# Hybrid encoder with a mixture of experts: router logits one tile later among the output products, and gate-weight splitting and loading in other places

## What is computed

```python
mix = jnp.concatenate([o_mla, o_d], axis=-1) @ w_o
x = layer_norm(ALPHA * x + mix, ln1_g, ln1_b)            # x1
scores = jax.nn.sigmoid(xt @ w_router)                   # the logits: 768 x 16
# top-1 of 4 groups, top-2 experts inside it, gates = scores / sum
for e in range(N_EXPERTS):
    h = jax.nn.silu(xt @ w_gate[e]) * (xt @ w_up[e])
    y = y + gates[:, e:e + 1] * (h @ w_down[e])
x = layer_norm(ALPHA * x + y, ln2_g, ln2_b)
```

## Time and profile before

| | |
|---|---|
| runs | 829.7, 826.49, 824.76 us; median 826.49 us |
| profiled execution | 825.78 us |
| its span in the trace | 823.9 us (1.9 us lie around it) |
| busy in the span | PE 722.7 us (88%), weight loads 600.3 (73%), DVE 582.2 (71%), ACT 482.4 (59%), POOL 264.6 (32%) |
| DMA | 185.71 MB, mean 225 GB/s |

### The profile page before, as it was taken

How to read it: one execution, slowest core, us unless ns; L and a number is a source line. 1 busy time by engine, 2 the same in 40 slices (tenths; PEclk the granted TensorE clock), 3 DMA queues, 4 the chain that set the end, 5 groups by cost and what they waited for, 6 DMA issues and landing times. The chain is left out here.

```text
span 823.9 us, 12546 instructions
## 1 busy us (share of the span) xinstructions
PE 722.7 (88%) x3751; PEld 600.3 (73%) x3751; DVE 582.2 (71%) x970; ACT 482.4 (59%) x864; POOL 264.6 (32%) x292
## 2 busy tenths in 40 slices
PE   4999989998999699999996499999999999999830
PEld 3898878886778477767785377888887777777620
DVE  6874445555555766785775779898998888888608
ACT  3334345545554655775127157887888788887505
POOL 3133166555654232334410114132222222232101
PEclk9999999999999879999995599999999999999965
DMA  9714220222025863311835759999999999999735
GB/s 346 254 69 154 89 77 9 70 64 64 2 65 176 263 247 115 111 34 67 322 150 195 255 173 377 393 394 390 373 389 394 392 394 393 393 394 392 243 89 242
DMA packets 71912, 185.71 MB, mean 225 GB/s; under 512 B 10560, under 2 KB 26944, under 8 KB 71872
## 3 DMA queue, kind: packets, MB, share of 16 engines
q1 hardware_dynamic: 66976, 167.38, 53.0%
q0 software_dynamic: 4896, 17.83, 8.4%
HBM read 153.20 MB, written 31.98 MB: 225 GB/s over the span
## 5 line engine op out<-in xcount | busy, mean ns | idle before, releaser
L2228 DVE TENSOR_TENSOR eDl<-rawD,eDh 128x1024 fp32r<-128x1024 f32 x68 | 80.2, 1220 | 12.3 <-ACT eDh L2172 12.1
L1265 POOL TENSOR_SCALAR me<-me,mrec 128x512 f32<-128x512 f32 (+1 forms) x48 | 65.0, 1355 | 57.0 <-DVE mrec L1444 57.0
L2228 DVE TENSOR_TENSOR eUl<-rawU,eUh 128x1024 fp32r<-128x1024 f32 x68 | 78.8, 1220 | 5.0 <-ACT eUh L2172 2.6
L2228 DVE TENSOR_TENSOR eGl<-rawG,eGh 128x1024 fp32r<-128x1024 f32 x64 | 75.9, 1222 | 7.4 <-ACT eGh L2172 6.9
L2300 POOL DMA_INDIRECT acc_rows<-yg,idx_s x17 | 31.3, 1841 | 147.8 <-ACT yg L2197 147.8
L2172 ACT ACTIVATE eGh<-rawG 128x1024 fp32r<-128x1024 f32 x64 | 65.5, 1058 | 8.1 <-DMA rawG<-in_w_gate 7.2
L1071 ACT ACTIVATE pT_h<-bank 128x512 fp32r<-128x512 f32 (+1 forms) x48 | 25.3, 527 | 75.4 <-PE bank L781 75.4
L1450 DVE TENSOR_TENSOR pT_l<-bank,pT_h 128x512 fp32r<-128x512 f32 (+1 forms) x48 | 28.9, 601 | 50.6 <-ACT pT_h L1071 50.6
L2120 PE MATMUL bank<-eGh,xgT_h 128*128 128x512 f32 x136 | 56.8, 418 | 8.5 <-DVE xgT_l L2233 7.4
L2172 ACT ACTIVATE eDh<-rawD 128x1024 fp32r<-128x1024 f32 x64 | 64.0, 1055 | 0.0
L2172 ACT ACTIVATE eUh<-rawU 128x1024 fp32r<-128x1024 f32 x64 | 62.3, 1050 | 0.0
(11 more groups left out here) (323 smaller groups left out, 2114.3 us busy)
## 6 DMA issues: line engine op xcount, KB each, us to landing
rawG<-in_w_gate SPq DMA_DIRECT2D x68, 512.0 KB, 15.3
rawU<-in_w_up SPq DMA_DIRECT2D x68, 512.0 KB, 12.4
rawD<-in_w_down SPq DMA_DIRECT2D x68, 512.0 KB, 13.6
wb_raw<-in_w_in SPq DMA_DIRECT2D x8, 512.0 KB, 4.7
wo_raw<-in_w_o SPq DMA_DIRECT2D x8, 512.0 KB, 7.4
acc_rows<-ax SPq DMA_DIRECT2D x7, 512.0 KB, 2.6
xln_rows<-res SPq DMA_DIRECT2D x6, 512.0 KB, 3.8
dqk_high<-st_h SPq DMA_DIRECT2D x8, 384.0 KB, 2.3
```

Of the source, the lines that this page charges most:

```text
L1265: nc.gpsimd.tensor_scalar(e, e, mrec[:, g % NSB:g % NSB + 1], None, ALU.mult).then_inc(m_p, 1)
L2228: nc.vector.tensor_tensor(wl_[X][i][:], raw_of(X, t, i)[:], f32(wh_[X][i][:]), ALU.subtract).then_inc(s_lo[X], 1)
```

## The change

There are two `x1T` tiles (at 202 and 42 KB) and two pairs of banks, (0, 1) and (5, 6), used in turn. On PE turn_x1(t) moves to the place ahead of the products of tile t+2 for t = 0 and behind those of tile t+1 for the others, and logits(t-1) follows turn_x1(t): turn_x1(0); products of tile 2, turn_x1(1), logits(0); products of tile 3, turn_x1(2), logits(1); products of tile 4, turn_x1(3), logits(2); products of tile 5, turn_x1(4), logits(3), logits(4), turn_x1(5), logits(5). turn_x1(1) waits in addition for the last readers of banks 5 and 6 in attention.

ACT makes the high parts of gate pieces 0 to 2 before its wait for the zero rows, and that of piece 3 behind the router's exponential and the last `ax`. DVE makes the low part of piece 0 between the two adds of tile 4, that of piece 1 between those of tile 5, that of piece 2 behind the layer norm of tile 5, and that of piece 3 behind `gate_vals`, at the very end of the block. SP issues pieces 0 to 2 of the second expert and 0 to 2 of the third, and then piece 3 of the second expert and, once that has landed, piece 3 of the third. Numbers of instructions and bytes stay as they are.

```diff
--- before.py
+++ after.py
@@ -381,7 +381,8 @@
     ln1g_sb = at("ln1g_sb", 30, [P, D])
     ln1b_sb = at("ln1b_sb", 34, [P, D])
     ax = [at(f"ax{i}", (38, 198)[i], [P, D]) for i in range(2)]
-    x1T = at("x1T", 202, [P, KD, P])
+    x1T = [at(f"x1T{i}", (202, 42)[i], [P, KD, P]) for i in range(2)]
+    X1_BANKS = ((0, 1), (5, 6))
 
     raw = {X: [at(f"raw{X}{i}", 78 + 16 * n + 4 * i, [P, 2 * FF]) for i in range(4)] for n, X in enumerate("GUD")}
 
@@ -1674,16 +1675,15 @@
                 sp.wait_ge(s_stored[i], 16 * (NT // 2))
             sp.wait_ge(s_x1st, 16 * NT)
 
-            for i in range(4):
-                sp.wait_ge(s_lo["G"], i + 1)
-                sp.dma_start(unit_dst("G", i), unit_src("G", 1, i)).then_inc(s_raw["G"][i], 16)
-
-
             sp.wait_ge(s_o, 24)
             sp.wait_ge(s_log, NT)
-            for i in range(4):
-                sp.wait_ge(s_raw["G"][i], 32)
-                sp.dma_start(unit_dst("G", i, 2), unit_src("G", 2, i)).then_inc(s_raw["G"][i], 16)
+            for units in (range(3), range(3, 4)):
+                for i in units:
+                    sp.wait_ge(s_lo["G"], i + 1)
+                    sp.dma_start(unit_dst("G", i), unit_src("G", 1, i)).then_inc(s_raw["G"][i], 16)
+                for i in units:
+                    sp.wait_ge(s_raw["G"][i], 32)
+                    sp.dma_start(unit_dst("G", i, 2), unit_src("G", 2, i)).then_inc(s_raw["G"][i], 16)
 
         @block.tensor
         def _(pe):
@@ -1693,11 +1693,15 @@
                 pe.wait_ge(s_x1, t + 1)
 
                 pe.wait_ge(s_bias, 2 * DT)
-                wait(pe, s_x1e, 2 * t)
+                if t == 1:
+                    pe.wait_ge(s_ptl, DT)
+                    pe.wait_ge(s_otl, DT)
+                wait(pe, s_x1e, 2 * t - 2)
                 for hf in range(2):
                     for j in range(4):
                         c = 4 * hf + j
-                        last = nc.tensor.transpose(psum[hf][:, j * P:(j + 1) * P], res[:, t, c * P:(c + 1) * P], ident[:])
+                        last = nc.tensor.transpose(psum[X1_BANKS[t % 2][hf]][:, j * P:(j + 1) * P], res[:, t, c * P:(c + 1) * P],
+                                                   ident[:])
                     last.then_inc(s_x1t, 1)
 
             def logits(t):
@@ -1705,20 +1709,16 @@
                 pe.wait_ge(s_rt, 32)
                 pe.wait_ge(s_y, 12)
                 for c in range(KD):
-                    last = nc.tensor.matmul(psum[2][:, t * NE:(t + 1) * NE], x1T[:, c, :], wr_sb[:, c, :],
+                    last = nc.tensor.matmul(psum[2][:, t * NE:(t + 1) * NE], x1T[t % 2][:, c, :], wr_sb[:, c, :],
                                             start=(c == 0), stop=(c == KD - 1))
                 last.then_inc(s_log, 1)
 
-            for k in range(16, 18):
-                front_o_part(k, 0, 12)
             turn_x1(0)
-            for t in range(3, NT):
+            for t in range(2, NT):
                 front_o_part(12 + 2 * t, 0, 12)
                 front_o_part(13 + 2 * t, 0, 12)
-                logits(t - 3)
-                turn_x1(t - 2)
-            logits(NT - 3)
-            turn_x1(NT - 2)
+                turn_x1(t - 1)
+                logits(t - 2)
             logits(NT - 2)
             turn_x1(NT - 1)
             logits(NT - 1)
@@ -1757,28 +1757,30 @@
                     act.wait_ge(s_raw[X][i], 16)
                     nc.scalar.activation(wh_[X][i][:], raw[X][i][:], ACT.Copy).then_inc(s_hi[X], 1)
 
+            def scaled(t):
+
+                if t >= 2:
+                    act.wait_ge(s_stored[t % 2], 16 * (t // 2))
+                nc.scalar.activation(ax[t % 2][:], res[:, t, :], ACT.Copy, scale=ALPHA).then_inc(s_ax, 1)
+
+            act.wait_ge(s_o, 12)
+            high0("G", range(3))
             act.wait_ge(s_zst, 32)
             for t in range(NT):
-                if t == NT - 1:
-
-                    act.wait_ge(s_o, 24)
-                    high0("G", range(3))
                 act.wait_ge(s_x1, t + 1)
-
-                if t >= 2:
-                    act.wait_ge(s_stored[t % 2], 16 * (t // 2))
                 for hf in range(2):
                     act.wait_ge(s_x1t, 2 * t + hf + 1)
 
-                    wait(act, s_log, t)
-                    nc.scalar.activation(x1T[:, 4 * hf:4 * hf + 4, :], psum[hf][:].rearrange("p (c n) -> p c n", c=4),
-                                         ACT.Copy).then_inc(s_x1e, 1)
-                if t == NT - 1:
-                    high0("G", range(3, 4))
-                nc.scalar.activation(ax[t % 2][:], res[:, t, :], ACT.Copy, scale=ALPHA).then_inc(s_ax, 1)
+                    wait(act, s_log, t - 1)
+                    nc.scalar.activation(x1T[t % 2][:, 4 * hf:4 * hf + 4, :],
+                                         psum[X1_BANKS[t % 2][hf]][:].rearrange("p (c n) -> p c n", c=4), ACT.Copy).then_inc(s_x1e, 1)
+                if t < NT - 1:
+                    scaled(t)
             act.wait_ge(s_log, NT)
             nc.scalar.activation(sg[:], psum[2][:, 0:NT * NE].rearrange("p (t e) -> p t e", t=NT), ACT.Exp,
                                  scale=-1.0).then_inc(s_rexp, 1)
+            scaled(NT - 1)
+            high0("G", range(3, 4))
 
 
             act.wait_ge(s_x1st, 16 * NT)
@@ -1842,8 +1844,15 @@
         def _(dve):
             front_dve(dve)
             dve.wait_ge(s_ln1w, 32)
+
+            def low0(i):
+                dve.wait_ge(s_hi["G"], i + 1)
+                nc.vector.tensor_tensor(wl_["G"][i][:], raw["G"][i][:], f32(wh_["G"][i][:]), ALU.subtract).then_inc(s_lo["G"], 1)
+
             for t in range(NT):
                 for hf in range(2):
+                    if hf and t >= NT - 2:
+                        low0(t - (NT - 2))
                     k = 12 + 2 * t + hf
                     ns = slice(hf * HW, (hf + 1) * HW)
                     dve.wait_ge(s_o, k + 1)
@@ -1860,9 +1869,8 @@
                 nc.vector.scalar_tensor_tensor(out=res[:, t, :], in0=res[:, t, :], scalar=rstd[:, t:t + 1], in1=ln1b_sb[:],
                                                op0=ALU.mult, op1=ALU.add).then_inc(s_x1, 1)
 
-            for i in range(4):
-                dve.wait_ge(s_hi["G"], i + 1)
-                nc.vector.tensor_tensor(wl_["G"][i][:], raw["G"][i][:], f32(wh_["G"][i][:]), ALU.subtract).then_inc(s_lo["G"], 1)
+            dve.wait_ge(s_o, 24)
+            low0(2)
 
             tt, ts = nc.vector.tensor_tensor, nc.vector.tensor_scalar
             stt, reduce = nc.vector.scalar_tensor_tensor, nc.vector.tensor_reduce
@@ -2009,6 +2017,7 @@
             for j in range(3):
                 last = tt(gate_vals[:, :, j, :], in_tile[:], gate_part[:, j, :].unsqueeze(2).to_broadcast(full), ALU.mult)
             last.then_inc(s_gvals, 1)
+            low0(3)
 
 
 
```

## The result

| | before | with the change |
|---|---|---|
| median | 826.21 us (6 runs, 824.76 to 829.7) | 829.54 us (6 runs, 827.66 to 832.29) |
| ratio, 95% interval | | 1.0043 (1.0023 to 1.0062) |
| profiled execution | 825.78 us | 831.65 us |
| its span | 823.9 us | 829.8 us |

The kernel is 0.43% slower, some 3.5 us. The forecast was +1.4 us; 829.54 lies in its range and within 0.5%, but the interval leaves 1 out, and two and a half times the predicted size asks for a cause.

The account below looks back on a forecast made before the run. Full DMA from about 490 us bounds the kernel, so the second block's start counts: the router comes 1.7 us earlier, but SP's late piece 3 opens the barrier 1.4 us later; 826.5 + 1.4 = 827.9 us, range 824.8 to 830.8.

Parts of the forecast that it names:

- The bound: Expert stage: DMA engines full from about 490 us, so the end follows the second block's start, set by the first block's barrier.
- One of the signs of being wrong: From the barrier to the kernel's end: the prediction is wrong if this distance changes by more than a us.
- The late piece 3: End of first block: SP loads it only after DVE's late low part, landing 3.5 us, so the barrier opens 1.4 us later.
- close: From the start of gate_vals to the barrier's opening; predicted opening 467.3 us, with SP last instead of POOL.
- The rivals in which SP isn't last: At the first block's barrier: SP not last or hardly later than POOL, gain kept, down to -1.7, 824.8 us; chance 0.08.
- The slow lone load: SP's wait for piece 3: landing takes 6.4 us, barrier opens 4.3 us later, 830.8 us, +0.5%; chance 0.09.
- The wait for the zero rows: On PE ahead of logits(0): ACT's copies wait for the zero-row store, so PE stands 1.7 us, from 408.3 to 410.0.
- the shift stays: On PE from k = 18 (first output product behind logits(0)): +3.9 us, kept through the later rounds to the last product.
- The predicted tail: From x1 of tile 0 ready, 400.70 us, to the end of the router's exponential, predicted at 445.4 us.
- The forecast's -1.7 for the tail: Router's chain on DVE: starts at 445.4 us, 1.7 us earlier than before, so gate_vals ends at 462.0.
- The clock rival: PE, last tile: clock falls 3 us later, turn and logits save 2.6 us, +1.4 becomes -1.2, 825.3 us; chance 0.12.
- the 5.9 us behind the last product of the prediction: PE's clock falls some 5.9 us behind the last 512-column product, at 439.3 us, so the last tile runs at low clock.

Follow-up runs that it names:

- r_after: The changed kernel, unedited, run once more for a second profile; 829.34 us (1 run).
- e5: Kernel before with only the low part of piece 3 put behind gate_vals and SP's loads in the change's order; 830.20 us, ratio 1.0048 to before.
- e1: Changed kernel with gate piece 3's high part, low part and loads put back early, new PE order kept; 827.49 us, ratio 1.0014 to before.
- e3: Changed kernel with both edits, piece 3 early again (e1) and the zero-row wait moved later (e2); 822.79 us, ratio 0.9968 to before.
- e8: e2 with the load of the third expert's gate piece 3 moved into the second block; 822.67 us, ratio 0.9950 to before.
- e2: Changed kernel with ACT's wait for the zero-row stores moved from before the x1T copies to before the first write into ax1; 824.56 us, ratio 0.9989.
- e7: Changed kernel with 12 unused 512-column products on PE between turn_x1(1) and logits(0); 827.11 us, ratio 1.0013 to before.
- e9: e3 with 8 unused 512-column products on PE, 4 ahead of logits(3) and 4 ahead of logits(4); 820.99 us, and 821.81 when run again.
- e10: e9 with 2 more unused products ahead of turn_x1(5) and 3 ahead of logits(5); 821.47 us, ratio 0.9948 to before.

## Why the prediction was right in direction and short in size

- **The bound: right.** The kernel's end is the barrier's opening plus 357.1 to 359.4 us, in every profile. One of the signs of being wrong did appear in the first pair, where this distance changed by 1.3 us (357.9 to 359.2); the second pair, 358.3 and 358.4, shows that it was spread between executions.
- **The late piece 3: right, mechanism and size.** Predicted were a landing of 3.5 us, SP last and a close of 467.3 - (462.37 - 1.7) = 6.6 us; measured 3.2 us (3.1 in r_after), SP last by 2.7, a close of 6.4. e5 shows it alone, e1, e3 and e8 its absence. The estimate of 3.2 us from the Trainium skill, "DMA: Bandwidth & Descriptors", under "Anatomy of one DMA — SWDGE (gpsimd) path", was the better of the two: the trace agrees with it to 0.1 us, although this load is SP's and not GpSimd's. The rivals in which SP isn't last are out.
- **The slow lone load** (6.4 us) did not come: its row came from a load that shared the queues with two stores.
- **The wait for the zero rows: seen, but taken as a constant.** The 1.7 us came out as 1.88 and 1.61. It is not a constant: the stores stand behind eight loads on SP's queue (one was 13.1 us on its way before), and their landing moved by 1.8 us between the profile after and e1, PE's arrival by 3.4, so an execution that comes early waits longer (3.50 us in e1) and loses part of its head start.
- **The step that failed** is the sentence that from k = 18 on "the shift stays" at +3.9 us, with 1.7 for the wait: it priced the wait at its own length. I asked for the clock only behind the last product. In two of three profiles it fell in or behind the wait, which cost 1.8 us on top of the wait's 1.88 in the profile after (11.9 - 8.2 - 1.88) and 4.7 on top of 3.50 in e1 (16.4 - 8.2 - 3.5). The predicted tail was 445.4 - 400.7 = 44.7; r_after, with the clock up, has 45.1, the first profile 47.0. The mechanism of the new order was right, and its price without the wait is -3.1 us (e3, e8); with it, it is anything from -1.3 to +5.1 in three profiles.
- **The sum.** +2.8 for the close; for the tail -1.3, +0.6 and +5.1 in the three profiles with the wait. That makes +1.5, +3.4 and +7.9, and the measured +3.5 lies among them. Over all executions the terms are -3.1 for the new order (from the profiles), +4.5 for the wait (e2, by the ratios) and +2.8 for the close, in sum +4.2, which fits the measured 3.5 within its interval (1.9 to 5.1). The forecast's -1.7 for the tail was the best case taken as the likeliest. That 829.54 still lay in the range was partly luck: the upper end of 830.8 stood for the slow lone load, and what moved the time was a clock that fell behind the wait, which had no rival of its own.
- **The clock rival** ("stays up for the last tile") did not come: turn_x1(5) and logits(5) ran at the low clock in both profiles of the changed kernel (1.97 and 3.60 us in the first). The rule on transposes from the Trainium skill, "TensorE: Matmul & The Clock Gate", under "Part 4: PE-mode transpose", which the prediction weighed beside it, is not contradicted. The clock even fell earlier than the 5.9 us behind the last product of the prediction, some 3.9 us (at 440.8) and 3.4 us (at 438.8 in r_after), amid logits(4); that cost nothing there, since those logits were done before x1 of the last tile was ready.

## What to carry to other kernels

Before an instruction is moved ahead on its engine, list what each wait in its way waits for; one that was covered by the work now behind it, here for stores that the copies have nothing to do with, becomes a stall, and such a wait belongs ahead of the first instruction that truly needs it. Nothing should wait for a DMA's landing between the last computed value and a barrier: issue the second load in the next block. A stall of PE between dense products is dearer than its length, since the granted clock can fall for the products behind it.

## What the runs showed of the hardware

- An idle stretch of 1.88 us on PE, between groups of transposes and 16-column products, was followed two us later by some 3 us at 1.2 GHz amid dense products (first profile after). In one of 3.50 us (e1) the clock fell before the stretch ended and was low for some 10 us; one of 1.61 us (r_after) brought no low clock. With dense but useless products in its place the clock stayed at 2.4 GHz, in the one profile taken (e7).
- With useless products in the tail the place where the clock fell differed between executions: ahead of turn_x1(5) without them (e3), ahead of logits(5) and behind it in the two profiles of e9, and amid logits(4) in e10, whose instructions up to there are those of e9.
- A lone load of 512 KB (128x1024 fp32), issued by SP, took 3.1 to 3.2 us from issue to landing (after, r_after, e2, e5, e7, e8), while the same load as one of four issued together took up to 7.0 us.
- POOL's drain at the end of a block lasted 4.8 to 5.1 us when an indirect gather had been issued just ahead of it, in all 14 profiles. That the drain waits for the gather was not tried.
